# Two-layer hybrid decoder trunk: VectorE forms the low parts of the streamed weight slabs, GpSimd only rounds

## What is computed

```
h = rms_norm(x, ln_mix_pre);  p = h @ w_in            # p is cut into the inputs of three mixers and gates
y_a = dsa_attention(...)       # indexer scores, top 128 of the causal keys of each query, softmax, 4 heads
y_b = gated_delta_rule(...)    # short conv + SiLU, chunked triangular solve, state scan, norm, SiLU gate
y_c = retention(...)           # fixed decay per head, norm, swish gate
merged = gates[0] * (y_a @ w_ba) + gates[1] * (y_b @ w_bb) + gates[2] * (y_c @ w_bc)
x = x + rms_norm(merged @ w_out, ln_mix_post)
x = x + rms_norm(square(relu(rms_norm(x, ln_mlp_pre) @ w_up)) @ w_down, ln_mlp_post)
```

## Time and profile before

| | |
|---|---|
| median of three runs | 2002.19 us (2001.02 to 2003.47) |
| the profiled execution, whole time | 2001.97 us |
| its span, first to last instruction | 2000.2 us |
| PE busy | 1928.5 us |
| DVE, POOL, ACT busy | 1067.6, 1024.3, 474.2 us |

### The profile page before, as it was taken

How to read it: one execution, slowest core, us unless ns; L and a number is a source line. 1 busy time by engine, 2 the same in 40 slices (tenths; PEclk the granted TensorE clock), 3 DMA queues, 4 the chain that set the end, 5 groups by cost and what they waited for, 6 DMA issues and landing times.

```text
span 2000.2 us, 25269 instructions
## 1 busy us (share of the span) xinstructions
PE 1928.5 (96%) x8926; PEld 1552.1 (78%) x8926; DVE 1067.6 (53%) x1686; ACT 474.2 (24%) x923; POOL 1024.3 (51%) x821
## 2 busy tenths in 40 slices
PE   8999999999999999999999999999999999999998
PEld 7876667788778888888878667677887788888887
DVE  5754798743464550363366547987435646403623
ACT  3153243221323100011222533523113241000111
POOL 5663443335670666666346534342456607666662
PEclk9999999999999999999999999999999999999999
DMA  6332112222520322222222311122125204222321
GB/s 241 133 122 68 56 61 71 80 74 74 200 95 1 138 95 95 95 98 92 84 85 95 127 58 64 63 72 79 64 74 210 84 1 147 94 95 97 102 93 57
DMA packets 72475, 186.77 MB, mean 93 GB/s; under 512 B 18304, under 2 KB 30784, under 8 KB 71488
## 3 DMA queue, kind: packets, MB, share of 16 engines
q1 hardware_dynamic: 41328, 152.10, 22.2%
q10 hardware_dynamic: 31056, 33.38, 5.0%
HBM read 174.40 MB, written 11.06 MB: 93 GB/s over the span
## 4 chain that ended last, share of the span: by engine, by line
PE 77%; DVE 15%; ACT 4%; issue 3%; POOL 1%; DMA 0%; DVEq 0%; SPq 0%; POOLq 0%; ACTq 0%
PE psD L1008 19%; PE psD L1009 19%; PE psD L1010 19%; PE psM L1008 3%; PE psM L1009 3%; PE psM L1010 3%; DVE work L2047 3%; DVE small L2045 3%; PE psM L1067 2%; PE psM L1074 2%; PE psM L1164 1%; PE psM L1172 1%; DVE x L1946 1%; POOL w_lo L982 1%; ACT wide L1508 1%
## 5 line engine op out<-in xcount | busy, mean ns | idle before, releaser
L982 POOL TENSOR_TENSOR w_lo<-raw,w_hi 128x1024 fp32r<-128x1024 f32 x272 | 672.8, 2473 | 22.7
L1008 PE MATMUL psD<-a_hi,w_hi 128*128 128x512 f32 (+2 forms) x1488 | 601.3, 404 | 10.0 <-DVE a_lo L2170 6.6
L1010 PE MATMUL psD<-a_hi,w_lo 128*128 128x512 f32 (+2 forms) x1488 | 578.4, 389 | 0.0
L1009 PE MATMUL psD<-a_lo,w_hi 128*128 128x512 f32 (+2 forms) x1488 | 578.3, 389 | 0.0
L977 POOL TENSOR_TENSOR w_hi<-raw,tabs 128x1 fp32r<-128x1 f32 x272 | 62.7, 230 | 916.9 <-PE psD L1010 806.7
L1008 PEld LDWEIGHTS psD<-a_hi,w_hi 128*128 128x128 f32 (+1 forms) x1488 | 281.9, 189 | 89.8 <-issue 30.2
L1009 PEld LDWEIGHTS psD<-a_lo,w_hi 128*128 128x128 f32 (+1 forms) x1488 | 281.9, 189 | 59.7 <-issue 5.7
L1010 PEld LDWEIGHTS psD<-a_hi,w_lo 128*128 128x128 f32 (+1 forms) x1488 | 281.5, 189 | 58.8 <-issue 0.4
L978 POOL TENSOR_SCALAR w_hi<-raw 128x1023 fp32r<-128x1023 f32 x272 | 297.8, 1095 | 0.0
L2200 DVE TENSOR_TENSOR f_lo<-gt,f_hi 128x512 f32 x64 | 127.4, 1990 | 59.3 <-ACT f_hi L1766 59.3
L1766 ACT CAST f_hi<-gt 128x512 f32 x64 | 39.8, 622 | 479.7 <-DVE gt L2197 479.7
(11 more groups left out here) (268 smaller groups left out, 2720.7 us busy)
## 6 DMA issues: line engine op xcount, KB each, us to landing
raw<-in_ws SPq DMA_DIRECT2D x272, 512.0 KB, 3.2
s_raw<-in_wo ACTq DMA_DIRECT2D x14, 512.0 KB, 11.4
out<-x SPq DMA_DIRECT2D x8, 512.0 KB, 5.5
x<-rows_d ACTq DMA_DIRECT2D x4, 1024.0 KB, 6.8
x<-out ACTq DMA_DIRECT2D x2, 2048.0 KB, 8.2
e_raw<-in_wo ACTq DMA_DIRECT2D x8, 512.0 KB, 6.5
tabs<-in_tab SPq DMA_DIRECT2D x1, 2944.0 KB, 11.4
x<-in_x SPq DMA_DIRECT2D x4, 512.0 KB, 5.3
```

The lines of the kernel that those rows point to most:

```text
L982: pool.tensor_tensor(w_lo[:, s, :], raw[:, s, :], w_hi[:, s, :].bitcast(F32), ALU.subtract) \
L1008: pe.matmul(out, lhi, rhi, start=start, stop=False)
L1009: pe.matmul(out, lhi, rlo, start=False, stop=False)
L1010: return pe.matmul(out, llo, rhi, start=False, stop=stop)
```

## The change

POOL keeps the rounding and loses the subtraction. The subtraction `raw - w_hi` is now a DVE instruction for every one of the 272 slabs, at a fixed place of DVE's order:

- the scheduler gets the durations hi = 1.35 (POOL's rounding) and lo = 1.25 (the new DVE step), `slow` goes from 1.3 to 1.05, each slab that PE ends adds a step ("dve", "lo", n) of the highest rank, and PE's first piece of a slab waits for it in the model;
- prefix and tail get the lo steps by a rule of `every`; the tail is also written anew: four gates of branch B come before its first merge instead of two, the splits of branch B after the third gate, and the stay steps near the end, two of them behind the last merge;
- in the MLP one lo stands in each of the 16 passes of `hidden`, eight ahead of `add_half0` and eight ahead of `add_half1`;
- one lo stands behind the four diagonals at the program's start, one behind the eight low parts of the normed input in each layer, and two behind the merge.

```diff
-    slow = 1.3
+    slow = 1.05
+    hi, lo = 1.35, 1.25
...
+    def rounded(n, at):
+
+        name = ("dve", "lo", n)
+        todo[name], rank[name], later[name], wants[name] = (lo, [("pool", "hi", n)], 0.0), 1e6, [], 0
+        end["pool", "hi", n] = at + hi - latency
+        open_["dve"].append(name)
...
+            if slabs + 1 > first_slab:
+                at = max(at, end.get(("dve", "lo", slabs + 1), 1e9) + latency)
...
-    tail = merges("B", 0)
-    for j in range(len(STAYING)):
-        tail.insert(3 + 2 * j, ("stay", j))
-    tail = [("split", "B", h) for h in range(H)] + tail
...
+    tail = [("mgate", "B", n) for n in range(3)] + [("split", "B", h) for h in range(H)]
+    stays = [("stay", j) for j in range(len(STAYING))]
+    tail += [("mgate", "B", 3), ("merge", "B", 0), ("mgate", "B", 4), ("mgate", "B", 5), ("merge", "B", 1), stays[0],
+             ("mgate", "B", 6), stays[1], ("mgate", "B", 7), stays[2], ("merge", "B", 2), *stays[3:5], ("merge", "B", 3), *stays[5:]]
...
+        def lo_slab(dve, n, of=None):
+
+            l = layer if of is None else of
+            s = (l * NSLAB + n) % 2
+            dve.wait_ge(*on("w_hi", n + 1, l))
+            if l or n > 1:
+                dve.wait_ge(*on("slab_done", n - 1, l))
+            dve.tensor_tensor(w_lo[:, s, :], raw[:, s, :], w_hi[:, s, :].bitcast(F32), ALU.subtract) \
+                .then_inc(*inc("split"))
...
-                def split(s):
+                def round_(s):
...
-                def rest(s):
-                    pool.tensor_tensor(w_lo[:, s, :], raw[:, s, :], w_hi[:, s, :].bitcast(F32), ALU.subtract) \
-                        .then_inc(sem("split"), 1)
...
                         pool.wait_ge(sem("slab_done"), it * 2 + (s - 1))
                         pool.wait_ge(sem(f"raw_in{s}"), it * 16 + 16)
-                        split(s)
-                        pool.wait_ge(sem("w_hi"), it * 2 + (s + 1))
-                        rest(s)
+                        round_(s)
...
+                        lo_slab(dve, 1)
...
+                    for n in range(2):
+                        lo_slab(dve, SL_MLP + n)
...
+                                lo_ahead(it * 4 + (first + i + 2), i + 2, FG // 4)
                                 dve.wait_ge(*on("f_hi", it * 4 + g * FG + (i + 1)))
...
+                    def lo_down(g, slabs):
+
+                        for m in slabs:
+                            lo_slab(dve, SL_MLP + g * PER_GROUP + FG + m + 2)
+
                     for g in range(GROUPS - 1):
                         hidden(g)
+                        lo_down(g, range(FG // 2))
                         add_half0(g)
+                        lo_down(g, range(FG // 2, FG))
                         for t in range(ST):
                             add_half1(g, t)
...
+                    lo_down(GROUPS - 1, range(FG // 2))
                     add_half0(GROUPS - 1)
```

More of the change, by code:

```diff
@@ L431, in schedule @@
                 dense += stage[n]
+                slabs += 1
+                rounded(slabs + 2, end[n])
         for m in later[n]:
@@ L436, in schedule, with every @@
     assert len(out) == len(todo)
-    tail = merges("B", 0)
-    for j in range(len(STAYING)):
-        tail.insert(3 + 2 * j, ("stay", j))
-    tail = [("split", "B", h) for h in range(H)] + tail
[L443 to L452, removed]
+    tail = [("mgate", "B", n) for n in range(3)] + [("split", "B", h) for h in range(H)]
+    stays = [("stay", j) for j in range(len(STAYING))]
+    tail += [("mgate", "B", 3), ("merge", "B", 0), ("mgate", "B", 4), ("mgate", "B", 5), ("merge", "B", 1), stays[0],
+             ("mgate", "B", 6), stays[1], ("mgate", "B", 7), stays[2], ("merge", "B", 2), *stays[3:5], ("merge", "B", 3), *stays[5:]]
+    def every(steps, n, ahead=()):
+        o, late = [], []
+        for s in steps:
+            o += [("pe", *s), ("act", *s)]
+            if s[0] in STREAMED:
+                o += late
+                late = []
+            o.append(("dve", *s))
+            if s[0] in STREAMED and s != ("rot", 4):
+                late.append(("dve", "lo", n + 2))
+                n += 1
+            if s[0] not in ("va", "silu", "unit_sq", "decays"):
+                o += late
+                late = []
+        return o
+    opened = every(prefix, 0)
+    opened.remove(("dve", "lo", slabs_before + 1))
+    closed = every(tail, slabs + 1)
+    closed.remove(max(s for s in closed if s[1] == "lo"))
+    return opened + out + closed
+STREAMED = ("misc", "conv", "va", "rot", "cv", "cg", "z", "gate", "mergeC", "mgate", "merge")
 ORDER = schedule()
@@ L591, in build @@
         layer = 0
-        per_layer = {"slab_done": NSLAB, "split": NSLAB, "a_hi": (2 + ST) * KT, "a_lo": (2 + ST) * KT,
+        per_layer = {"slab_done": NSLAB, "split": NSLAB, "w_hi": NSLAB, "a_hi": (2 + ST) * KT, "a_lo": (2 + ST) * KT,
                      "h_turned": KT, "r_pre_mix": ST, "diag_pre_mix": ST}
@@ L2188, in _, with lo_ahead @@
                     lo_x1(READY)
+                    def lo_ahead(n, s, times):
+                        s = (layer * NSLAB + SL_MLP + s) % 2
+                        dve.wait_ge(*on("w_hi", n + 1))
+                        dve.tensor_tensor(w_lo[:, s, :], raw[:, s, :], w_hi[:, s, :].bitcast(F32), ALU.subtract) \
+                            .then_inc(*inc("split", 1, times))
                     def hidden(g):
+                        first = SL_MLP + g * PER_GROUP
                         with dve.Fori(0, FG // 4) as it:
@@ L2249, in _ @@
                         gained2(t, 0)
+                    lo_down(GROUPS - 1, range(FG // 2, FG // 2 + 2))
+                    if layer < DEPTH - 1:
+                        lo_slab(dve, 0, layer + 1)
                     for t in range(ST):
```

7 lines of the change are left out of this document (5 added, 2 removed).

## The result

The changed kernel took 1986.34 us in the median of four runs (1983.23 to 1989.03), the one before 2002.83 beside it. The ratio is 0.9909, with a 95% interval from 0.989 to 0.9928: 16.5 us faster where 20 were forecast. The profiled execution took 1989.03 us with a span of 1987.2, that is 13.0 under the span of before.

What follows compares the result with a forecast made beforehand. PE, busy 1928.5 of 2000.2 us, was taken as the bound. Per layer 1 + 6.5 + 3 + 3.2 - 5.4 = 8.3, twice 16.6, plus 3 once: 19.6 off 2001.97 gives 1982, range 1960 to 2010.

Steps and rivals of the forecast that it cites:

- the likeliest case: Whole kernel: all goes as forecast, likeliest 1982 us, range 1974 to 1990; chance 0.50.
- the picking of the top keys: In the mix, 140 us from 228: VectorE loses less to locks, PE's loss falls from 14.5 to 8; gain 6.5 a layer.
- the end of the mix: Around the last merges: the 1.4 us wait at the splits goes, the last wait ends 1.7 earlier; gain 3 a layer.
- The turn of the groups: MLP, first to second group: the eighth w_lo delays the copy out of psD; PE waits 3.35 us, loss 5.4 a layer.
- The price of the subtraction: On VectorE: 272 subtractions at 1.21 us each, 329 us more; its busy time becomes 1160 to 1300 us.
- the balance of VectorE's time: In the picking: 125.5 us less about 10 plus 24.2 of w_lo makes 140; idle time falls from 14.5 to 10.
- the 256-column row: Sign on VectorE: its pr instruction on 256 columns, 0.84 us in the mean before, would be near 0.36.
- The change of layers: Between the layers, once: the one-column instruction's 2.27 us becomes 0.22, PE's wait 4.30 becomes 2.25; gain 3.
- the rotations: Before slab 22: VectorE's chain shortens, but about 2.4 us of PE's wait come back at slab 20; gain 1 a layer.
- The start of the MLP: PE's 1.20 us wait for POOL's subtraction goes, with 1.5 of clock and 0.45 of another wait; 3.2 a layer.

## Why the prediction was nearly right, and where it was not

**The total.** 1986.3 lies within the likeliest case's range (1974 to 1990), 4 over its figure. Part of that is luck. By the ledger, with its low clock counted in, the picking of the top keys gave 9.4 and 12.6 us in the two layers where 6.5 stood in the sum for each; the end of the mix gave next to nothing where 3 stood; and 5.2 us of slower matmuls were in no term. These errors nearly cancelled.

**The turn of the groups: right in place, chain and size.** 3.35 us were forecast and 3.30 measured in both layers, with the clock 5.0 and 6.4 where 5.4 stood in the sum. Undoing that one step gave 12.5 us back.

**The price of the subtraction: right.** 1.22 us in the median, 0.01 over the row from which it was taken. VectorE's busy time came to 1145.5, below the lower bound of 1160: 329 us more work took only 78 more, so some 250 us of held time went, where at most 237 had been counted on.

**The picking of the top keys: the failed step.** The prediction laid the gain there (6.5 a layer) to VectorE's instructions no longer being held behind POOL, read off. The gain came, and larger: 7.3 and 10.7 by the table, 9.4 and 12.6 with the low clock behind the last wait. The reason is refuted by two runs. With POOL subtracting as before in the new order the waits are 2.5 us; with VectorE subtracting in an order made without the steps' price they are 10.6. The term that was wrong is the balance of VectorE's time: 10 us of lock were taken off and 24.2 of w_lo put on, and then its idle time was let fall as if less waiting behind POOL would serve PE. Measured in one and the same order, over 165 us instead of the prediction's 140, the lock is 20.3 us and the w_lo 24.3, and PE's waits move by 0.3. What does change them is the order: the scheduler's model has a step of 1.25 us for each slab and places the other steps, and PE's pieces, with that in view. The single number slow = 1.05 gives part of it (6.0 us of waits). That the time so left in the order serves whatever holds VectorE, its own subtraction or POOL's, fits all four numbers but was not tried by itself. The prediction saw the long rows and did not ask whether they were on a path that PE waited for: in the new order with the old engine they are there too (2.37 us for negb on 256 columns), and PE's waits are short. In the changed kernel they went only in part, and POOL's rounding remains: the 256-column row has a mean of 565 ns now,

```profile
L2108 DVE TENSOR_SCALAR pr<-pr,small 128x256 f32<-128x256 f32 x4 | 2.3, 565 | 0.1
```

where 0.36 was to be seen.

**The change of layers: right.** 2.25 us against 2.25 forecast, and 3.0 in all. This, the start, the rotations, the end of the mix and POOL's waits in the MLP are where the old engine does cost: 24.6 us, by the run with the new order and the old engine.

**The rotations: half right.** The wait by the norms fell from 3.65 to 1.89, and 1.81 came back at slab 20, whose w_lo stands behind the third turn, where 2.4 were forecast: 3.7 for 3.65, and with the clock a gain of 0 to 1 where 1 was forecast. That the second wait was avoidable, since VectorE idled for 4.1 us just ahead of it, was not seen.

**The end of the mix: over-sized.** 3 were forecast a layer. The wait of 1.4 at the splits went; one of 1.13 of the same kind, on "issue", stands at 432 us in its place: PE goes on as VectorE ends the four y_lo of a branch's output, which stand behind a w_lo. Of the last merges' waits 4.05 became 2.93 in the first layer and 2.93 + 0.75 in the second, and the first was followed by a low clock. The forecast had the order of the steps right (w_lo and two s_lo ahead of the six a_lo) and took 2.2 us for that wait instead of 2.9.

**The start of the MLP: over-sized by its clock.** The 1.20 us wait for POOL went, to 0.03, as forecast. So did the 1.24 in the second group, of which the sum had nothing: it read the other waits on POOL's w_lo as 0.45 a layer, from one row of two. The 1.5 us of clock did not go: the waits of 2.57 and 0.73 us ahead of it stayed, and a low clock came in both layers, where before only the first had one.

**What was not in the sum.** Matmuls came 5.2 us slower in all, outside idle gaps and low clock. 4.2 of them are in the 96 recorded matmuls of the indexer scores, whose starts lie 0.23 us apart in the mean before and 0.28 after; but matmul records can be missing, and in the low clock those matmuls did not slow down like the large ones, which the ledger takes for granted. Whether this is a cost of the new interleaving or of the book-keeping stays open.

## What to carry to other kernels

A long duration on a helper engine is a loss only if the engine that bounds the kernel waits at the end of it: before such rows are put into a sum, look for the wait that they end, and to test the cause keep the order and exchange the engine, then keep the engine and exchange the order. When work moves onto an engine with a fixed order, its price must be in the model that makes the order (28 us here, for the prices of the step and of the rounding ahead of it), and every place where a hand-written piece puts the moved step ahead of the release of a buffer needs its own look (12.5 us here, for one step). On a TensorE-bound kernel, put a price on the clock behind a wait as well, but not in proportion to the wait: here it was mostly 1.4 to 3.1 us, or nothing (see below).

## What the hardware showed that was not expected

The same wait does not always bring the low clock. In the profiled run of the changed kernel the wait of 2.93 us at the end of the mix is in both layers, with the same work around it; the stretch at it in the first layer and in the second:

```profile
577.00:585.00 8.00, 5.07 (x17) 3.76 (x17) 7.97 (x12) 0.08 (x1) 1.96 (x2) 0.79 0.20 66
1561.00:1569.00 8.00, 5.07 (x23) 3.92 (x22) 7.96 (x12) 0.02 (x1) 1.96 (x2) 1.00 0.19 66
```

PE is busy for 5.07 us in both, with a granted clock of 0.79 and of 1.00. Over whole runs it shows as two groups of times: 1983.2 and 1983.9 with a mean granted clock of 0.992, 1988.8 and 1989.0 with 0.989. The profiles of all twelve kernels, without the program's start, bear this out. Of 17 waits of 2.0 to 2.3 us 6 had a low clock at or close behind them, of 28 of 2.5 to 2.7 us 18, and of 33 of 3.0 us or more all. What it cost by the ledger hardly depends on the wait: 2.6 us behind 2.39, 1.7 and 3.1 behind 3.30, 1.9 and 2.0 behind 6.15.

And taking out a short wait that stands close behind another gave at least as much in the clock as in idle time: at slab 20, 3.6 us of waits and 4.0 of clock for the two layers.
